# State-space layer: kernel rows and causal matrix stored with the group index innermost

## The reference, cut to what matters

```
bu   = u @ Bbar_g                      # u: 512 x 16 per group
x_t  = Abar_g * x_(t-1) + bu_t         # 64 complex states per group
y_t  = Re(C_g x_t) + d * u_t           # 16 outputs per group
out  = gelu(y) @ w_out ...             # then two gated halves
```

## Time and profile before

| what | us |
|---|---|
| median of three executions | 2630.32 |
| the profiled execution, its own time | 2631.51 |
| its span in the trace | 2629.7 |
| time outside the span | 1.8 |
| PE busy in the span | 2584.1 |
| the state-space steps with the changed parts | about 50 to 143 of the span |

### The profile page before, as it was taken

The page is one execution under the profiler, slowest core; times in us unless marked ns, Lnnn a source line. Parts: engine busy times, 40 slices in busy tenths (PEclk is TensorE's granted clock), DMA queues, the critical chain, the costliest instruction groups (busy, mean ns, idle before and its releaser), DMA issues.

```text
span 2629.7 us, 38280 instructions
## 1 busy us (share of the span) xinstructions
PE 2584.1 (98%) x15944; PEld 2190.6 (83%) x15944; DVE 1438.2 (55%) x2165; ACT 1050.4 (40%) x1560; POOL 120.2 (5%) x147
## 2 busy tenths in 40 slices
PE   6999999999999999999999999999999999999998
PEld 3789888888898888888888888988888988988887
DVE  8676555565463333365555555844336767834335
ACT  4734222233242222255555555533223564522323
POOL 6810000000000000000000000000000000000000
PEclk8999999999999999999999999999999999999999
DMA  7583555423322222322222222132222122222220
GB/s 259 90 325 129 192 192 192 184 73 97 112 97 96 96 96 98 110 74 73 73 76 82 73 80 86 54 128 96 96 96 81 55 91 90 104 96 96 96 96 33
DMA packets 55241, 286.89 MB, mean 109 GB/s; under 512 B 7154, under 2 KB 17666, under 8 KB 29091
## 3 DMA queue, kind: packets, MB, share of 16 engines
q1 hardware_dynamic: 49106, 241.98, 27.6%
q0 software_dynamic: 5968, 42.52, 4.3%
HBM read 278.19 MB, written 2.10 MB: 107 GB/s over the span
## 4 chain that ended last, share of the span: by engine, by line
PE 90%; DVE 5%; ACT 2%; DMA 1%; issue 1%; SPq 1%; POOL 0%; ACTq 0%; DVEq 0%
PE PS L728 18%; PE PS L729 18%; PE PS L730 18%; PE PS L862 4%; PE PS L864 4%; PE PS L863 4%; PE PS L821 1%; PE PS L820 1%; PE PS L819 1%; PE PS L891 1%; PE PS L892 1%; PE PS L893 1%; PE PS L948 1%; PE PS L754 1%; PE PS L755 1%; PE PS L756 1%
## 5 line engine op out<-in xcount | busy, mean ns | idle before, releaser
L728 PE MATMUL PS<-Hl,Wh 128*128 128x512 f32 x1256 | 489.0, 389 | 0.8 <-DVE Wl L1762 0.7
L729 PE MATMUL PS<-Hh,Wl 128*128 128x512 f32 x1256 | 488.7, 389 | 0.0
L730 PE MATMUL PS<-Hh,Wh 128*128 128x512 f32 x1256 | 488.6, 389 | 0.0
L1270 ACT CAST Wh<-raw 128x2048 fp32r<-128x2048 f32 (+2 forms) x152 | 273.8, 1846 | 403.1 <-PE PS L730 380.7
L1762 DVE TENSOR_TENSOR Wl<-raw,Wh 128x2048 fp32r<-128x2048 f32 (+1 forms) x158 | 342.5, 2207 | 63.7 <-ACT Wh L1270 62.9
L729 PE MATMUL PS<-Gh,Wl 128*128 128x512 f32 x848 | 329.9, 389 | 0.0
L730 PE MATMUL PS<-Gh,Wh 128*128 128x512 f32 x848 | 329.9, 389 | 0.0
L728 PE MATMUL PS<-Gl,Wh 128*128 128x512 f32 x848 | 329.9, 389 | 0.0
L728 PEld LDWEIGHTS PS<-Hl,Wh 128*128 128x128 f32 x1256 | 235.7, 188 | 50.4 <-DVE Wl L1762 1.4
L730 PEld LDWEIGHTS PS<-Hh,Wh 128*128 128x128 f32 x1256 | 235.7, 188 | 48.9
L729 PEld LDWEIGHTS PS<-Hh,Wl 128*128 128x128 f32 x1256 | 235.7, 188 | 48.8
(11 more groups left out here) (490 smaller groups left out, 4702.1 us busy)
## 6 DMA issues: line engine op xcount, KB each, us to landing
raw<-wstream SPq DMA_DIRECT2D x152, 1024.0 KB, 6.2
raw<-wstream SPq DMA_DIRECT2D x64, 768.0 KB, 4.5
adab<-adaw POOLq DMA_DIRECT2D x28, 1024.0 KB, 5.3
adah<-adaw POOLq DMA_DIRECT2D x12, 1024.0 KB, 7.1
raw<-wstream SPq DMA_DIRECT2D x20, 512.0 KB, 3.8
raw<-adap SPq DMA_DIRECT2D x4, 1024.0 KB, 10.7
ada_land<-adap SPq DMA_DIRECT2D x4, 1024.0 KB, 18.9
MT<-KPX SPq DMA_DIRECT2D x64, 64.0 KB, 2.8
```

What stands on the lines that cost most here:

```text
L728: mm(o, Wh[:, s, c0:c0 + P], xl[:, k, :], start=k == 0, stop=False)
L729: mm(o, Wl[:, s, c0:c0 + P], xh[:, k, :], start=False, stop=False)
L730: last = mm(o, Wh[:, s, c0:c0 + P], xh[:, k, :], start=False, stop=k == kt - 1)
L1270: nc.scalar.copy(w_high(p, h, widths[h]), raw[:, h, 0:widths[h]]).then_inc(split_h, 1)
```

## The change

The strip `KP` and the matrix `MT` change their order inside a partition from (group, position) to (position, group). The same bytes lie in the same tensors; for one position the values of the 8 groups are now next to each other.

- The ACT copy writes its 1024 values per partition in the same order of iteration as before (group by group, position running fastest), so consecutive values go 8 elements (32 bytes) apart instead of side by side. It reads PSUM as before.
- Each of the eight transfers reads and writes, per partition, one run of 1024 values (4 KB) instead of 8 runs of 128 values (512 bytes). Their number, bytes, partitions and waits are the same.
- The products of `s5_chunks` read `MT`, their moving operand, 8 elements apart: 128 columns per group at a stride of 32 bytes.
- The zeros of the strip are one run of 896 values on each partition instead of 8 runs of 112.

```diff
-        KP = KPX[0:16, :].rearrange("p (g n) -> p g n", g=8)
+        KP = KPX[0:16, :].rearrange("p (n g) -> p n g", g=8)
@@
+        MTN = [MT[:, b, :, :].rearrange("p g n -> p (g n)").rearrange("p (n g) -> p n g", g=8) for b in range(2)]
@@ SP
-                    sp.dma_start(MT[16 * j:16 * j + 16, t % 2, :, :], KP[:, :, 16 * j:16 * j + P]).then_inc(s5_s["mt"], 16)
+                    sp.dma_start(MTN[t % 2][16 * j:16 * j + 16, :, :], KP[:, 16 * j:16 * j + P, :]).then_inc(s5_s["mt"], 16)
@@ PE, s5_chunks
-                        last = mm(PS[64 * e:64 * e + 64, 5, i * P:(i + 1) * P], U_s[:, t % 4, 4 * e + i, :], MT[:, t % 2, 4 * e + i, :],
+                        last = mm(PS[64 * e:64 * e + 64, 5, i * P:(i + 1) * P], U_s[:, t % 4, 4 * e + i, :], MTN[t % 2][:, :, 4 * e + i],
                                   start=False, stop=True, skip_group_check=True)
@@ ACT, s5_k
-                nc.scalar.copy(KP[:, :, 112:240], PS[0:16, 2:4, :].rearrange("p b (i n) -> p (b i) n", i=4)).then_inc(s5_s["kc"], 1)
+                nc.scalar.copy(KP[:, 112:240, :].rearrange("p n g -> p g n"), PS[0:16, 2:4, :].rearrange("p b (i n) -> p (b i) n", i=4)).then_inc(s5_s["kc"], 1)
@@ POOL
-            g_.memset(KP[:, :, 0:112], 0.0).then_inc(s5_s["kz"], 1)
+            g_.memset(KP[:, 0:112, :], 0.0).then_inc(s5_s["kz"], 1)
```

## The result

| | before | after |
|---|---|---|
| median of 15 executions each, us | 2631.14 | 2636.60 |
| lowest to highest | 2629.37 to 2633.43 | 2635.73 to 2638.50 |
| ratio after / before, 95% interval | | 1.0020 [1.0014, 1.0027] |
| span of the profiled execution | 2629.7 | 2636.5 |
| PE busy in it | 2584.1 | 2591.7 |

The change costs 5.5 us between medians (3.7 to 7.1 by the interval). The remaining 1.3 lie after it and are less than the 4.1 us by which the 15 executions of the kernel before differ among themselves.

A forecast was written before the change was run, and what follows sets the result against it. PE, busy 98% of the span, was taken as the bound. Steps summed -0.7 + 1.1 + 0.9 + 0.5 + 2.2 + 0.9 = +4.9 us, giving a 2635.2 us median; range 2629.5 to 2651.

The forecast's parts named there:

- copy of the strip: ACT copy writing at 32 bytes' distance: 1.10 us more than its 1.00, so 2.10 us.
- products of a step: PE products reading at 32-byte stride: 0 to 1.05 us more per step, upper end taken, 2.1 us.
- an issue: Each transfer issue on SP: 0.43 us instead of 0.60, 1.36 us less per step over eight.
- landing: Time until the last transfer has landed: 2.2 us instead of 2.82, ends 1.9 and 2.82.
- products of step 0: First products: copy 1.10 us later, transfers 2.0 earlier, so start 0.9 us earlier; clock stays low, net -0.7.
- The larger is paid, not the sum: Copy and products, both awaited by `Yi`, still end at nearly the same time; only the larger delay lengthens a step.
- Which of the two shows: PE idle about 1.1 us behind line 592 in steps 1, 2, 4 and 5, with `Yi` on ACT as releaser.
- Steps 2 and 3: Transfer waits of 0.1 and 0.53 us before the products go: +0.9 us in step 2, +0.5 in step 3.
- Step 7: Its 1.0 us more of products is hidden by line 639's 0.97 us wait for the cast: no loss.
- The rival without cost: Stride costs nothing on ACT or within PE's pace, only transfers change: -2.7 us, 2627.6 us; chance 0.12.
- the one with halves in turn: Column halves no longer run side by side, products 3.8 us per step: +20.3, 2650.6 us; chance 0.17, in turn or part.
- the third: Transfers get no faster (0.60 and 2.82 us) while the copy takes 2.10: +6.9, 2637.2 us; chance 0.13.

The follow-up runs named there:

- experiment 4: Changed kernel with groups in pairs, values 8 bytes apart, transfer runs of 1 KB: 2631.66 us against 2631.65 for the kernel before, ratio 0.9998.
- experiment 5: Changed kernel with groups in fours, values 16 bytes apart, transfer runs of 2 KB: 2636.81 us against 2632.73 for the kernel before, ratio 1.0020.
- experiment 1: Changed kernel, but the products read MT densely as before (values then wrong): 2636.67 us against 2631.65 for the kernel before, ratio 1.0019.
- experiment 2: Changed kernel, but the ACT copy writes the strip densely and reads PSUM at a 512-byte stride: 2634.95 us, ratio 1.0014 to the kernel before.
- experiment 7: Kernel before with its layout, but four of step 0's eight transfers issued from ACT: 2631.69 us against 2632.73, ratio 0.9997.
- experiment 9: Changed kernel with copy and products dense (values wrong), 4 KB transfers kept, step 0's issued half from ACT: 2629.60 us against 2631.87 before, ratio 0.9990.
- experiment 6: Changed kernel with only the products of the first four groups per step, one column half: one execution, 2640.11 us; eight matmuls took as long as sixteen.

## Why the prediction was right

The prediction gave 2635.2 us, 4.9 above the median then known, 2630.32. Measured were 2636.60, which is 6.3 above that and 5.5 above the kernel before timed beside it. First the sizes:

| part | predicted | measured |
|---|---|---|
| copy of the strip | 2.10 us | 2.02 |
| products of a step | 2.1 | 2.06 |
| an issue | 0.43 | 0.59 |
| landing | 2.2 | 2.4 median (2.8 before), 2.48 in step 0 |

Then the sum, by marks on PE's timeline. The prediction counts a step up to the moment at which `Yi` is there, so the mark is the start of the turning back (line 657 before, 658 after); the growth is what a mark adds to how late the one above it is.

| mark | before | after | later by | growth | predicted |
|---|---|---|---|---|---|
| products of step 0 | 60.68 | 60.69 | 0.01 | 0.0 | -0.9 |
| turning back, step 0 | 63.64 | 63.77 | 0.13 | +0.1 | +0.2 |
| step 1 | 73.21 | 74.31 | 1.10 | +1.0 | +1.1 |
| step 2 | 82.45 | 84.29 | 1.84 | +0.7 | +0.9 |
| step 3 | 92.08 | 94.63 | 2.55 | +0.7 | +0.5 |
| step 5 (steps 4 and 5) | 110.12 | 114.59 | 4.47 | +1.9 | +2.2 |
| line 683 (684) after step 6 | 120.50 | 125.55 | 5.05 | +0.6 | +0.9 |
| line 639 (640) of step 7 | 142.76 | 148.26 | 5.50 | +0.4 | 0 |

- **Scattered access.** Both rates came out near the nearest rows. The copy's extra 1.02 us over 1024 values is 1.0 ns each, where line 1295 against line 1596 gave 1.07. For the products the row did not decide it: line 572's 1.88 ns per column could have been all weight load, as the prediction says, and the upper end was taken by likeness to the writes. It was right (1.7 to 1.8 ns), by a guess more than by a reading. Experiments 4 and 5 agree with the lines of 16 bytes that the Trainium skill's page Advanced Engine Details and Errata, section SBUF Cachelines, has: two values in a line were nearly free, one was not. The page gives no size for the penalty; the size is the trace's.
- **The larger is paid, not the sum.** This was the step on which the total hung. Experiments 1 and 2 show it from both sides: 1.0019 with the copy's cost alone, 1.0014 with the products' alone, 1.0020 with both.
- **Which of the two shows.** The prediction looked for 1.1 us of idle PE behind the transposes. It isn't there, because the two ends fell within 0.03 us of each other. Only experiment 1 has that gap.
- **The transfers** were mis-sized in both terms. An issue depends little on the runs: 589 ns for one run per partition against 600 for eight. The row of 0.43 us, a load into 128 partitions, was the wrong neighbour. The saving was also counted eight times where it could come seven times, since the landing of the earlier trace rows is counted from the start of the eighth issue. The landing was taken for a matter of packets, each with a time of its own whatever it carries; a packet's mean time rose from 0.059 to 0.20 us, and experiments 7 and 9 show a rate of 81 to 97 GB/s. The 0.9 us that step 0 should have gained were 0.0 in this trace.
- **Steps 2 and 3.** The wait before the products of step 2 had been 0.2 us, not 0.1, and went. That before step 3 went from 0.53 only to 0.29 us, where the prediction had it gone, since the round from copy to landing did not shrink to 8.1 us: it took 10.2 there (copy 2.03 from 81.66, seven issues in 4.3, landing 3.79 from 88.05). Why that landing is longer than the median of 2.4 is open. So a wait for transfers still mattered once, against what the prediction said.
- **Step 7** lost part of its cover: the wait of line 640 went from 0.97 to 0.43 us, with 0.97 us more of products before it, so only 0.54 was hidden. The wait hangs on a cast of weights on ACT (line 1413 before, 1414 after), which itself waits for a transfer into `raw`; it began at 139.69 before and at 145.19 after, 5.50 us later, while the products before it moved by 5.07.

The errors have both signs and leave 0.6 us: the start of step 0 was off by 0.9, and the other terms, together 0.3 too large, took some of that back. That it is no more is luck in part, since the two traces with the same copy and transfers and a long issue start the products of step 0 later still, counted from the copy. The two terms that carry the result, the 1 us per step and its being paid once, were right. The rival without cost falls by the durations, the one with halves in turn by the products' 2.06 us and by experiment 6, and the third was right in part: the transfers hardly improved (0.59 and 2.48 us instead of 0.60 and 2.82).

## What to carry to other kernels

Before making a transfer's runs longer, look at who writes and who reads the same tile. Here two engines each took 1 us more in every step for values 16 bytes or more apart, in exchange for fewer packets, and the number of packets was hardly a limit. Where an instruction waits for two inputs that end together, slowing either costs in full and slowing both costs once. Moving fewer bytes (with the largest blocks first) gained what moving them in fewer packets did not.

## What was not expected of the hardware

- Transfers between two sets of 16 partitions, issued from two queues, moved at 81 GB/s with packets of 512 bytes and at 97 with packets of 4 KB, where loads into 128 partitions reached 427 GB/s.
- ACT read PSUM at a stride of 512 bytes as fast as densely (1.002 us for 1024 values), while its writes to SBUF at 16 or 32 bytes took 2.0 us.
- A float32 matmul whose moving values lie 32 bytes apart runs at 1.7 to 1.8 ns per column, and two in different column halves still run side by side.
